# Two-block transformer step on one core: the first feed-forward streams a tile's high and low part as one product of 512 columns

## The reference, cut to what matters

```python
D_MODEL = 1024; SEQ = 256; D_FF = 4 * D_MODEL
...
        h = rmsnorm(x, norm_ffn_g[l])
        x = x + jnp.square(jax.nn.relu(h @ w_ff1[l])) @ w_ff2[l]
```

## Time and profile before

| | us |
|---|---|
| median of the runs | 942.65 |
| all runs | 953.18, 942.65, 941.45 |
| the profiled execution | 941.14 |
| its span, first to last instruction | 939.4 |
| PE busy / DVE busy / ACT busy in the span | 917.0 / 648.6 / 532.4 |

### The profile page before, as it was taken

How to read it: one execution, slowest core, us unless ns; L and a number is a source line. 1 busy time by engine, 2 the same in 40 slices (tenths; PEclk the granted TensorE clock), 3 DMA queues, 4 the chain that set the end, 5 groups by cost and what they waited for, 6 DMA issues and landing times.

```text
span 939.4 us, 18534 instructions
## 1 busy us (share of the span) xinstructions
PE 917.0 (98%) x7481; PEld 896.0 (95%) x7481; DVE 648.6 (69%) x1090; ACT 532.4 (57%) x868; POOL 0.2 (0%) x4
## 2 busy tenths in 40 slices
PE   7999999889999999999999999999999999999997
PEld 7999988889999999999999999999999999999996
DVE  8898768676656656766666457677769777776653
ACT  6888777676545645644444345445675565555451
POOL 0000000000000000000000000000000000000000
PEclk9999999999999999999999999999999999999999
DMA  9643334155666555555555454554515556555641
GB/s 309 207 166 106 102 130 142 62 165 199 219 214 192 183 180 180 179 180 180 180 180 179 158 172 138 165 166 132 175 46 170 184 171 218 180 185 202 218 137 45
DMA packets 110500, 157.30 MB, mean 167 GB/s; under 512 B 8656, under 2 KB 61776, under 8 KB 110416
## 3 DMA queue, kind: packets, MB, share of 16 engines
q1 hardware_dynamic: 110416, 156.12, 51.5%
HBM read 155.05 MB, written 1.05 MB: 166 GB/s over the span
## 4 chain that ended last, share of the span: by engine, by line
PE 90%; DVE 5%; ACT 3%; issue 1%; DVEq 0%; ACTq 0%
PE ps L1031 27%; PE ps L1029 27%; PE ps L1030 27%; DVE wl L1770 2%; PE ps L1068 1%; ACT wh L1354 1%; PE ps L1101 1%; PE ps L1043 1%; ACT U L1439 1%; DVE ACC L1810 0%; PE ps L1276 0%; PE ps L1296 0%; PE ps L1234 0%; PE ps L1297 0%; PE ps L1256 0%
## 5 line engine op out<-in xcount | busy, mean ns | idle before, releaser
L1770 DVE TENSOR_TENSOR wl<-raw,wh 128x1024 fp32r<-128x1024 f32 (+1 forms) x291 | 344.7, 1210 | 179.7 <-ACT wh L1354 179.5
L1029 PE MATMUL ps<-U,wh 128*128 128x256 f32 (+2 forms) x1408 | 404.1, 287 | 5.2 <-DVE wl L1770 5.2
L1354 ACT ACTIVATE wh<-raw 128x1024 fp32r<-128x1024 f32 (+1 forms) x291 | 296.9, 1045 | 183.8 <-PE ps L1031 182.6
L1031 PE MATMUL ps<-U,wl 128*128 128x256 f32 (+2 forms) x1408 | 397.2, 282 | 0.0
L1030 PE MATMUL ps<-UL,wh 128*128 128x256 f32 (+2 forms) x1408 | 396.1, 281 | 0.0
L1029 PEld LDWEIGHTS ps<-U,wh 128*128 128x128 f32 (+1 forms) x1408 | 264.3, 188 | 9.4 <-DVE wl L1770 6.9
L1030 PEld LDWEIGHTS ps<-UL,wh 128*128 128x128 f32 (+1 forms) x1408 | 263.7, 187 | 2.6 <-issue 1.2
L1031 PEld LDWEIGHTS ps<-U,wl 128*128 128x128 f32 (+1 forms) x1408 | 263.7, 187 | 0.5
L1029 PE MATMUL ps<-H,wh 128*128 128x256 f32 (+1 forms) x736 | 208.1, 283 | 0.4 <-DVE wl L1770 0.3
L1031 PE MATMUL ps<-H,wl 128*128 128x256 f32 (+1 forms) x736 | 206.2, 280 | 0.0
L1030 PE MATMUL ps<-HLO,wh 128*128 128x256 f32 (+1 forms) x736 | 205.7, 279 | 0.0
(11 more groups left out here) (324 smaller groups left out, 817.3 us busy)
## 6 DMA issues: line engine op xcount, KB each, us to landing
raw<-w_ff SPq DMA_DIRECT2D x64, 512.0 KB, 4.4
raw<-ffn_w_gate SPq DMA_DIRECT2D x88, 256.0 KB, 3.7
raw<-ffn_w_up SPq DMA_DIRECT2D x88, 256.0 KB, 4.6
raw<-ffn_w_down SPq DMA_DIRECT2D x44, 512.0 KB, 4.4
raw<-w_in SPq DMA_DIRECT2D x40, 512.0 KB, 4.4
raw<-w_out SPq DMA_DIRECT2D x16, 512.0 KB, 3.7
raw<-wkv_x SPq DMA_DIRECT2D x8, 512.0 KB, 3.5
raw<-w_in SPq DMA_DIRECT2D x9, 256.0 KB, 3.1
```

Of the source, the lines that this page charges most:

```text
L1029: e.matmul(out, sh, xh, start=(i == 0 and n == 0), stop=False)
L1031: mm = e.matmul(out, sl, xh, start=False, stop=(over and n == nk - 1))
L1354: e.activation(wh, raw, ACT.Copy).then_inc(*up("w_hi", v))
L1770: e.tensor_tensor(wl, raw, wh.bitcast(F32), ALU.subtract).then_inc(*up("w_lo", v))
```

## The change

For the stages `ff1a`, `ff1b`, `ff2a` and `ff2b` the products L1029 and L1030 become one: the high weight block stays loaded once and 512 columns stream, 256 of the high and 256 of the low activation, into the two halves of the bank. The third product goes into the first half as before. The bank then holds two sums. The evacuation of an ff1 tile copies the second half to a scratch, adds the first half, and then does what it did before, three instructions that each wait for the one before. The evacuation of an ff2 tile adds the second half to `X`, then the first, two instructions.

So that one access reaches both parts, `U` and `UL` become two views of one array `U_UL`, and `H` and `HLO` of one array `H_HLO`; the small tiles `ACC` and `RM` move behind them. The distances of the parts in the memory stay the same modulo 1024 bytes.

```diff
+PAIRED = ("ff1a", "ff1b", "ff2a", "ff2b")
+
+def streamed_pair(t, name, k):
+    return t["U_UL" if name in ("ff1a", "ff1b") else "H_HLO"][:, :, T1 * k:T1 * k + T1]
...
             sh, sl = wh[:, n, off:off + m], wl[:, n, off:off + m]
+            if name in PAIRED:
+                e.matmul(ps[:, 0:2 * T1], sh, streamed_pair(t, name, k), start=(i == 0 and n == 0),
+                         stop=(over and n == nk - 1), skip_group_check=True)
+                mm = e.matmul(out, sl, xh, start=False, stop=(over and n == nk - 1), skip_group_check=True)
+                continue
             e.matmul(out, sh, xh, start=(i == 0 and n == 0), stop=False)
             e.matmul(out, sh, xl, start=False, stop=False)
...
-            e.scalar_tensor_tensor(S(i, 0, T1), ps[:, 0:T1], 0.0, RS[:, 0:T1], ALU.max, ALU.mult).then_inc(
+            both = S(i, 2 * T2, 2 * T2 + T1)
+            e.tensor_copy(both, ps[:, T1:2 * T1]).then_inc(*up("low_sum", done))
+            e.wait_ge(*at("low_sum", done))
+            e.tensor_tensor(both, ps[:, 0:T1], both, ALU.add).then_inc(*up("both_sums", done))
+            e.wait_ge(*at("both_sums", done))
+            e.scalar_tensor_tensor(S(i, 0, T1), both, 0.0, RS[:, 0:T1], ALU.max, ALU.mult).then_inc(
                 *up("evacuated", done))
...
             xs = X[:, tag, T2 - T:T2]
+            if name in PAIRED:
+                e.tensor_tensor(xs, ps[:, T1:2 * T1], xs, ALU.add).then_inc(*up("low_sum", done))
+                e.wait_ge(*at("low_sum", done))
...
-        for n in ("U", "UL"):
-            t[n] = sb(n, [P, 8, T2], F32R)
+        t["U_UL"] = sb("U_UL", [P, 2, 8 * T2], F32R)
+        for i, n in enumerate(("U", "UL")):
+            t[n] = t["U_UL"][:, i, :].rearrange("p (k c) -> p k c", c=T2)
...
+        base_h, apart = nc.sbuf_base, 22 * T2 + 288
+        t["H_HLO"] = sb("H_HLO", [P, 2, apart], F32R)
```

More of the change, by code:

```diff
@@ L2447, in build @@
         t["G"] = sb("G", [P, 2, T2])
-        t["RM"] = sb("RM", [P, T2])
         beyond((base + 512) % 1024, 1024, "before_h")
[L2450 to L2455, removed]
+        base_h, apart = nc.sbuf_base, 22 * T2 + 288
+        t["H_HLO"] = sb("H_HLO", [P, 2, apart], F32R)
+        assert 4 * apart % 1024 == 512
+        top_h, top_hlo = base_h + 22 * T2 * 4, base_h + (apart + 22 * T2) * 4
+        for i, (n, beside, top) in enumerate((("H", "ACC", top_h), ("HLO", "RM", top_hlo))):
+            t[n] = t["H_HLO"][:, i, 0:22 * T2].rearrange("p (k c) -> p k c", c=T2)
+            t[beside] = nc.alloc_sbuf_tensor_at(beside, [P, T2], F32, offset=top)
         def over(top, *named):
```

## The result

| | before | after |
|---|---|---|
| median of the runs, us | 942.69 (4 runs, 941.45 to 953.18) | 958.75 (4 runs, 957.93 to 959.65) |
| the profiled execution, us | 941.14 | 957.93 |
| its span, us | 939.4 | 956.2 |

The changed kernel takes 1.0157 of the time before, interval 1.0116 to 1.0198: slower by 16 us, and inside the 2% that the prediction called no change. The forecast was 954.2 us, 4.6 too low, with the range 944 to 962. The sixteen runs of the kernel before that stand beside the later experiments fall into ten of 941.0 to 943.0 us and six of 947.0 to 948.7 us, so an excess of 5 or 6 us is read from profiles stage by stage, not from a single run.

A forecast was written before the change was run, and what follows sets the result against it. PE's stream of products was taken to bound the kernel, with DVE becoming the bound of ff1. 4.8 + 5.1 + 1.84 + 1.3 = 13.1 us, minus 0 on PE, on 941.14 gave 954.2 us, range 944 to 962.

The forecast's parts named there:

- DVE becomes the bound of ff1: In ff1, DVE's loop of 12.51 us a group exceeds PE's 10.88: 1.63 us a group once the slack is gone.
- The waits: PE waiting for DVE's splits: 4.8 us from ff1a, 5.1 from ff1b, 1.84 and 1.3 from ff2b's two groups.
- ff2b: Four extra adds of 0.46 us a group: 1.84 us in full, then 1.3 after 0.5 us of slack.
- No gain from fewer products: On PE in ff1 and ff2, a merged product costs what the two did: gain 0, counting 312 triples.
- The clock: Rival: PE's clock falls behind the new waits, 1.6 us each at four places, 6.4 us: 960.6 us; chance 0.12.
- Waits between DVE instructions at no cost: Rival: all four instructions of an ff1 tile take 0.33 us each, 3.5 us in all: 944.6 us; chance 0.11.
- The merged product that reads badly: Rival: streaming from two places makes a triple 360 ns against 340, 6.2 us on 312 triples: 960.4 us; chance 0.06.
- DVE keeps up: Rival: ff1 evacuation starts of 0.29 us or less add no wait there, and PE gains: 939.5 us; chance 0.07.

The follow-up runs named there:

- experiment 1: The changed kernel with three products of 256 columns again, keeping the changed evacuation: 956.57 us, ratio 1.0154 to the kernel before.
- experiment 4: The changed kernel with the change kept in ff2a and ff2b alone, ff1 as in the kernel before: 948.18 us, ratio 1.007 to the kernel before.
- experiment 6: The changed kernel with old evacuations, its merged product streaming two neighbouring high blocks from one piece of memory: 947.22 us, ratio 1.0034 to the kernel before.
- experiment 5: The changed kernel with the next ff1 tile's copy issued between a tile's add and its maximum: 952.51 us, ratio 1.0088 to the kernel before.
- experiment 3: The changed kernel's new arrays alone, with products and evacuations of the kernel before: 941.55 us, ratio 1.0011 to the kernel before.
- experiment 2: The changed kernel with the old evacuation, merged products kept and the bank's second half not read: 946.94 us, ratio 1.0056 to the kernel before.
- experiment 7: The changed kernel with the change kept in ff1a and ff1b alone, ff2 as in the kernel before: 953.96 us, ratio 1.0104 to the kernel before.

## Why the prediction was right, and where it was off

**DVE becomes the bound of ff1: right.** A tile of 1.58 us was forecast and 1.59 measured, a loop of 12.51 and 12.53. The dependent starts were priced from a place in another stage at 0.46 us, and the evacuation shows 0.45 and 0.46.

**The waits: right in place and number, 0.7 us too short, and their sum close partly by luck.** The forecast's 4.8, 5.1, 1.84 and 1.3 us add to 13.04 (it writes 13.1), and experiment 1, with PE's side undone, took 13.5 us of span more than the kernel before. But 0.25 of these lie ahead of `ff1a`'s first evacuation, and 0.4 are given back in `ff2b`'s second group, which the kernel before ran slowly; the waits are 5.3, 5.6, 1.84 and 0.9 to 0.95, 13.7 in all. The 0.5 missing in each half of `ff1` come for the most part from the first wait of each. The forecast took the moment at which ACT turns to the freed slot, 223.32 in `ff1a`, for the one at which PE needs the next split; PE starts that unit at 223.06 already. In experiment 1 PE starts it at 225.21, 2.15 us later, of which 0.24 it was late already at the start of `ff1a`: 1.9 us for the first wait, where 1.53 were forecast.

**ff2b: right for the first group, a little high for the second.** 1.84 us came in full, as forecast from a wait that stood there already. Of the second group's 1.84 I took 1.3 to come through, and 0.95 did, so the slack was 0.9 us, not 0.5.

**No gain from fewer products: right in its sign, wrong in its size. This is the term that was mis-sized.** I took 0 with bounds of -13.3 and +3.4 ns a triple; it is +13 (353 against 340). The upper bound came from one place with three products of 512 that run one behind the other, where 230 stands beside two of 115. Those rows had a sign of what was going on, since 115 isn't the 113.3 of the group's period, and I passed over it. The ratio of 2.0 held: a merged triple is 235 + 118, so the merged product costs two of the 256 product beside it. But that one has the slow pace too. The merged product isn't slower than two products of the slow pace; PE falls into that pace with it and stays there.

I had also counted 312 triples at PE's own pace. 164 count: the first 24 of `ff2a` and of `ff2b` lie ahead of a wait for DVE, behind the first evacuation of `ff1b` and of each group of `ff2b` DVE sets the pace, and `ff2b`'s second group was slow in the kernel before. 164 x 13 ns = 2.1 us. With 13.7 for the waits and 0.96 up to `ff1a`'s first evacuation the sum is 16.8, the difference of the spans. Of the 4.6 us by which the forecast was short, 2.1 are the slow triples, 1.0 the later start, 0.7 the waits, and 0.8 the distance of the changed kernel's median (958.75) from its profiled execution (957.93).

The Trainium skill, page "TensorE: Matmul & The Clock Gate", section "Back-to-back issue gap", gives N / 2.4 + 2.5 ns, and calls it the gap of an isolated product, which at few columns leaves out what the weight loads take in a stream. By it a merged pair would save 2.5 ns. The trace disagrees: a merged triple costs 13 ns more.

**The rivals.** The clock: it stayed at 1.00 behind waits of 0.8 to 1.7 us; only behind the one of 2.99 us ahead of `ff1a`, which the kernel before has with 2.69, PE ran at 1.2 GHz. The length of that wait doesn't decide it: in experiments 4 and 6 it was 2.99 and 2.98 us, and the granted clock stayed at 1.00 (190 to 200 us). Waits between DVE instructions at no cost: ruled out by 0.45 against 0.33 us and by experiment 5, where taking six of the eight away from each group made it 0.76 us shorter. That also speaks against the Trainium skill, page "VectorE: DVE Perf Modes", section "The DRAIN you can't avoid", which found eight copies with a semaphore after each no slower than eight with only one at the end. The merged product that reads badly: it was the right place, priced at 360 ns a triple where 353 were measured, but by the wrong cause; experiment 6 reads from one place and is as slow. DVE keeps up: in the groups of `ff1` shown here no start on DVE came under 0.33 us.

**What stays open.** Why PE has two paces for a product, what chooses one at a wait, and why PE falls into the slow one where a stage of 512 or of 272 columns begins. The DMA share doesn't choose: the slow `ff1b` of experiment 4 had 0.60 and the fast one before 0.57, and the slow stretch of experiment 3 had 0.55 where the fast one before had 0.60. Other distances between the high and the low part in the memory weren't tried. Each merged stage was seen slow in every profile taken (the changed kernel and experiments 2, 4, 5, 6 and 7, one execution each); that it can't run fast isn't shown. The long runs of the kernel before weren't profiled; that their 6 us are the slow pace too is argued from experiment 3's trace.

**No better version came out of this.** Of the kernels that merge all four stages and have complete sums, experiment 5 is the fastest that was run; merging `ff2` alone took 948.18 us (experiment 4), also more than the kernel before. The merged products alone cost more than the kernel before takes (experiment 2), so there is nothing to win by covering DVE's waits further.

## What to carry to other kernels

Merging two products that share their weights takes instructions away, not columns; here nothing came back for the instructions, and the second sum in the bank moved real work to DVE. Before adding to a feeding engine, write down its loop from start to start, with what it waits for in the middle, and compare it with the loop of the engine it feeds: of DVE's 2.8 us of idle time in 10.88 the 1.28 ahead of the splits were a wait for ACT that moved along, and only the other 1.49 were cover, for 3.2 us of new work. Where dependent instructions follow each other, put the next tile's independent one between them: with the same instructions that was worth 6.2 us of 16.

## What the runs showed of the hardware

- Products of 256 columns of this type run at 113.3 or at 118 ns at the same granted clock of 1.00, and keep their pace for tens of microseconds. The fast one is lost at a wait (0.25 us in the kernel before, while experiment 3's kernel kept it at the same place) or, with no wait, at the first product of 512 (experiments 4 and 7) or of 272 columns (experiments 1, 3 and 7). It came back at a wait: one of 0.98 us in experiment 7. In experiment 3's trace the slow pace in the second block makes 6.3 us of 942.
- A stage with products of 512 columns among those of 256 ran in the slow pace in all six kernels that had one, and left it to the unmerged stage behind it as long as no wait came between (experiments 4 and 7).
- At half the clock there is no such excess: the first triples of `ff1a` in the changed kernel take 0.64 us, which are 768 columns at 1.2 GHz.

```profile
191.82 0.62 PE L1039 MATMUL ps<-U_UL,wh 128*128 128x512 f32 x1 [2.99 <-DVE wl L1784]
...
195.01 0.61 PE L1039 MATMUL ps<-U_UL,wh 128*128 128x512 f32 x1
```

From 191.82 to 195.01 are five triples, 638 ns each.
